# Seven block products instead of eight in one half of a feed-forward input projection

## The chip, the cores and the metric

The kernel runs on one NeuronCore of a Trainium2 chip as one launch. The metric is the device time of that launch in microseconds (us). Five engines run their own instruction streams in order and meet at semaphores: PE (TensorE, matrix products into PSUM), DVE (VectorE), ACT (ScalarE), POOL (GpSimd) and SP (SyncE, which here issues the DMAs of the weights).

## The reference, cut to what matters

Two blocks of layers work on 256 tokens of a sequence `x` and 256 tokens of a context, D_MODEL = 1024, in float32. The change lies in the second block, layer 1, in the first of its two feed-forward networks, which handles both token sets (512 columns):

```python
D_FF = 2816
def swiglu(h, w_in, w_out):
    a, b = jnp.split(h @ w_in, 2, axis=-1)
    return (jax.nn.silu(a) * b) @ w_out
...
x = x + 0.5 * mx[:, 2] * swiglu(ada_norm(x, norm_g[l, 0], mx[:, 0], mx[:, 1]), ffn_w_in[l, 0], ffn_w_out[l, 0])
hctx = hctx + 0.5 * mc[2] * swiglu(ada_norm(hctx, norm_g[l, 0], mc[0], mc[1]), ffn_w_in[l, 0], ffn_w_out[l, 0])
```

`h @ w_in` is 512 tokens by 1024 by 5632. The kernel computes it in two halves of 11 gate chunks (columns of `a`) and 11 value chunks (columns of `b`), 128 columns each, with the output projection of each half behind it.

## The kernel before, in words

A phase list (`plan`) is walked by each engine; a phase of kind `gemm` is one weight matrix or part of one. Everything is kept transposed: features on the 128 partitions, tokens along the free axis. `h` is 8 chunks of 128 features by 512 tokens (256 of x, then 256 of the context).

Every operand is split into two float32r parts, `hi` (a rounded copy) and `lo` (value minus `hi`), and a product is three matmuls: hi by hi, hi by lo, lo by hi. A *unit* is one 128-column weight chunk: SP loads it from DRAM (512 KB) into one of four slots of `deep`, ACT copies it to `w_hi` (L1398), DVE subtracts to get `w_lo` (L1875), PE uses it. `w_hi` and `w_lo` are rings of RING = 4 units; ACT and DVE work LEAD = 3 units ahead of PE.

In the phase that the change replaces (evacuation `swiglu`, 22 units, alternately gate and value), PE runs for each unit 8 chunks x 3 parts x 2 token halves = 48 matmuls of 128x256 (L1063). For a pair of units ACT takes the gate's silu out of PSUM (L1450), DVE multiplies it with the value's PSUM bank into `gt` (L1904), rounds that to `g_hi` (L1908) and subtracts to get `g_lo` (L1910); `g` feeds the output projection. POOL does nothing there. Engines run a hardware loop of four units per round.

Ahead of it stands the output projection of the first half (evacuation `resid`, 8 output chunks of two units with 6 and 5 chunks of `g`, 66 matmuls each, the result added into `resid` by DVE, L1917). Behind it stands the output projection of the second half, whose matmuls read `g` chunk 10 as the last of their first output chunk.

## Time and profile before

| | us |
|---|---|
| runs of the kernel before, median of 3 | 2347.16 (2341.73 to 2347.69) |
| the profiled execution, whole | 2344.51 |
| its span | 2342.7 |
| PE busy in the span | 2249.8 (96%) |
| DVE, ACT, POOL busy | 1144.3, 855.9, 176.3 |
| first half's output projection on PE | 1695.17 to 1755.13 = 59.96 |
| second half's input projection on PE (replaced) | 1755.13 to 1875.03 = 119.90 |

The profile is of one execution. Its page gives busy time by engine, a chain of what ended last, and groups of instructions by source line. The trace behind it answers for any stretch of time: busy time of each engine, instructions in order, and what an engine waited for. Line numbers are those of the kernel before.

### The profile page before, as it was taken

The page shows a single profiled execution, that of the slowest core. Times are in us where ns is not written, and L with a number is a line of the kernel's source. Part 1 is how long each engine was busy: PE and PEld are TensorE (multiplying, and loading weights), DVE is VectorE, ACT ScalarE, POOL GpSimd, SP SyncE. Part 2 cuts the span into 40 slices and gives each one's busy share as a digit, 9 for nine tenths or more (in the row PEclk, how much of TensorE's full clock was granted, in tenths as well). Part 3 has the DMA queues.
Part 4 walks back from the last instruction along what each step waited for, and adds up shares of the span by engine and source line. Part 5 has one row for each costly group of instructions (what it writes and reads, how often), then busy time and mean ns, then how long its engine had stood idle before and what let it go on. Part 6 is the DMA issues. An engine that isn't in the chain of part 4 may idle for free.

```text
span 2342.7 us, 47206 instructions
## 1 busy us (share of the span) xinstructions
PE 2249.8 (96%) x19336; PEld 2107.6 (90%) x19336; DVE 1144.3 (49%) x1926; ACT 855.9 (37%) x1392; POOL 176.3 (8%) x150
## 2 busy tenths in 40 slices
PE   6999999899999999988999999999999999999998
PEld 4986798789999999976999999999999998968998
DVE  5226375653433445456653333354343345576665
ACT  4125454632221233248432222243222234356544
POOL 0003112100000010501200000010000010001000
PEclk9999999999999999998999999999999998999999
DMA  9653544444675343521364665243243233324573
GB/s 309 193 160 112 156 142 107 122 149 152 182 213 179 89 131 115 154 73 28 109 183 127 204 199 175 84 118 91 72 122 93 82 98 91 91 64 128 172 209 111
DMA packets 515886, 315.53 MB, mean 135 GB/s; under 512 B 16035, under 2 KB 513274, under 8 KB 515622
## 3 DMA queue, kind: packets, MB, share of 16 engines
q1 hardware_dynamic: 515160, 313.45, 45.6%
q8 instruction: 99, 1.62, 0.3%
q14 instruction: 37, 0.30, 0.0%
q10 hardware_dynamic: 590, 0.16, 0.0%
HBM read 312.50 MB, written 1.06 MB: 134 GB/s over the span
## 4 chain that ended last, share of the span: by engine, by line
PE 87%; DVE 7%; ACT 3%; issue 2%; DMA 1%; ACTq 0%; POOL 0%; DVEq 0%; POOLq 0%
PE ps L1063 65%; PE ps L1107 4%; PE ps L796 3%; PE ps L1010 3%; DVE w_lo L1875 2%; PE ps L980 2%; ACT w_hi L1398 1%; PE ps L938 1%; PE ps L2142 1%; PE ps L2126 1%; PE ps L907 1%; PE ps L869 1%; PE ps L2490 1%; PE ps L2165 1%; PE ps L2394 0%
## 5 line engine op out<-in xcount | busy, mean ns | idle before, releaser
L1063 PE MATMUL ps<-h_hi,w_hi 128*128 128x256 f32 x3424 | 742.2, 282 | 11.1 <-issue 3.6
L1063 PE MATMUL ps<-h_lo,w_hi 128*128 128x256 f32 x3424 | 733.6, 279 | 0.0
L1063 PE MATMUL ps<-h_hi,w_lo 128*128 128x256 f32 x3424 | 733.0, 279 | 0.0
L1063 PEld LDWEIGHTS ps<-h_hi,w_hi 128*128 128x128 f32 x3424 | 548.4, 189 | 32.0 <-issue 26.5
L1063 PEld LDWEIGHTS ps<-h_lo,w_hi 128*128 128x128 f32 x3424 | 549.1, 190 | 0.1
L1063 PEld LDWEIGHTS ps<-h_hi,w_lo 128*128 128x128 f32 x3424 | 549.1, 190 | 0.0
L1875 DVE TENSOR_TENSOR w_lo<-stage,w_hi 128x1024 fp32r<-128x1024 f32 x227 | 285.3, 1259 | 264.2 <-ACT w_hi L1398 264.1
L1398 ACT ACTIVATE w_hi<-stage 128x1024 fp32r<-128x1024 f32 x227 | 236.5, 1055 | 337.3 <-PE ps L1063 217.3
L1875 DVE TENSOR_TENSOR w_lo<-deep,w_hi 128x1024 fp32r<-128x1024 f32 x184 | 225.2, 1234 | 236.9 <-ACT w_hi L1398 235.3
L1398 ACT ACTIVATE w_hi<-deep 128x1024 fp32r<-128x1024 f32 x184 | 190.9, 1055 | 157.1 <-PE ps L1063 116.0
L1063 PE MATMUL ps<-g_hi,w_hi 128*128 128x256 f32 x1100 | 233.8, 281 | 0.8 <-DVE w_lo L1875 0.3
L1063 PE MATMUL ps<-g_hi,w_lo 128*128 128x256 f32 x1100 | 231.4, 279 | 0.0
L1063 PE MATMUL ps<-g_lo,w_hi 128*128 128x256 f32 x1100 | 231.2, 279 | 0.0
L1450 ACT ACTIVATE vtok<-ps 128x512 f32<-128x512 f32 (+1 forms) x82 | 44.3, 540 | 475.1 <-PE ps L1063 475.1
L1063 PEld LDWEIGHTS ps<-g_hi,w_hi 128*128 128x128 f32 x1100 | 173.9, 188 | 5.9 <-issue 4.0
L1063 PEld LDWEIGHTS ps<-g_hi,w_lo 128*128 128x128 f32 x1100 | 174.0, 189 | 0.0
L1063 PEld LDWEIGHTS ps<-g_lo,w_hi 128*128 128x128 f32 x1100 | 173.5, 188 | 0.0
L1540 DVE TENSOR_REDUCE modT<-ps 128x16 f32 (+1 forms) x88 | 12.0, 171 | 218.3 <-PE ps L807 218.3
L1958 POOL MEMSET vtok<- 128x512 f32 x6 | 3.2, 527 | 1205.1 <-PE ps L1063 1205.1
L796 PE MATMUL ps<-modw,svec 128*32 128x256 f32 x1408 | 89.7, 386 | 0.0
L1904 DVE TENSOR_TENSOR vtok<-vtok,ps 128x512 f32<-128x512 f32 (+1 forms) x82 | 50.2, 612 | 73.8 <-PE ps L1063 73.8
L1917 DVE SCALAR_TENSOR_TENSOR resid<-ps,modA,resid 128x256 f32<-128x256 f32 (+1 forms) x120 | 53.5, 479 | 52.3 <-PE ps L1063 52.3
(406 smaller groups left out, 2896.4 us busy)
## 6 DMA issues: line engine op xcount, KB each, us to landing
modw<-in_ada_w SPq DMA_DIRECT2D x72, 1024.0 KB, 6.9
stage<-in_ffn_w_in SPq DMA_DIRECT2D x88, 512.0 KB, 3.9
deep<-in_ffn_w_in SPq DMA_DIRECT2D x88, 512.0 KB, 3.9
modw<-in_w_mod SPq DMA_DIRECT2D x18, 1024.0 KB, 8.3
stage<-in_w_in SPq DMA_DIRECT2D x30, 512.0 KB, 5.2
stage<-in_ffn_w_out SPq DMA_DIRECT2D x32, 384.0 KB, 3.3
stage<-in_even_w_in SPq DMA_DIRECT2D x24, 512.0 KB, 4.1
deep<-in_ffn_w_out SPq DMA_DIRECT2D x32, 384.0 KB, 3.3
```

Source lines behind the costliest of these rows:

```text
L796: last = mm(ps[32 * j:32 * j + 32, 4, 0:SEG], svec[:, m["block"], k, lhs], modw[:, par, k, :], start=par == 0 and k < 4, stop=par == 1 and ...
L869: last = mm(half_sums(v)[:, a * 64:(a + 1) * 64], part[:, a * P:(a + 1) * P], ones[:, 0:64], start=first and a + n == 0, stop=final and n ...
L907: last = mm(ps[:, k, cols], w_part[wp][:, (u0 + k) % RING, c, :], x_part[xp][:, c, cols], start=n == 0 and wp == xp, stop=n == KC - 1 and ...
L980: last = mm(ps[:, 2 + j, cols], w_part[wp][:, u % RING, n, :], t_part[xp][:, x, cols], start=x == 0 and wp == xp, stop=x == sum(ks) - 1 an ...
L1010: last = mm(ps[:, bank, part], w_part[wp][:, u % RING, n, :], x_part[xp][:, n, cols], start=n == 0 and wp == xp and (k["dst"] is not None ...
L1063: last = mm(ps[:, j, v - a:v - a + SEQ], w_part[wp][:, u % RING, c, :], x_part[xp][:, x, v:v + SEQ], start=first and wp == xp and v == a, ...
L1107: last = mm(ps[:, bank, (tile % 2) * SEQ:(tile % 2) * SEQ + SEQ], x_part[xp][:, c, tile * P:(tile + 1) * P], w_part[wp][:, u % RING:u % RI ...
L1398: up(act(w_hi[:, u % RING], slot, ACT.Copy), "w_hi", rounds)
L1450: up(act(sg[:, j // 2, 0:n], ps[:, j, 0:n], ACT.Silu), f"bank_free{j}", rounds)
L1875: up(V.tensor_tensor(w_lo[:, u % RING], arrival(u)[0], w_hi[:, u % RING].bitcast(F32), ALU.subtract), "w_ready", rounds)
L1904: up(V.tensor_tensor(gt[:, 0:n], sg[:, j // 2, 0:n], ps[:, j, 0:n], ALU.mult), f"bank_free{j}", rounds)
L1917: last = V.scalar_tensor_tensor(rs, ps[:, j, v * SEQ:(v + 1) * SEQ], gate[:, bass.ds(i * 8 + at, 1)], rs, ALU.mult, ALU.add)
```

## The change

The weights of one gate chunk and one value chunk form, with the two halves of the 1024 features, a 2 by 2 block matrix: A11 and A12 (gate; features 0 to 511, 512 to 1023), A21 and A22 (value). The tokens form B11, B12 (features 0 to 511 of x and of the context) and B21, B22. A block product is 128x512 by 512x256, 4 chunks x 3 parts = 12 matmuls. The plain result takes eight block products; the new phase `cells` takes seven, after Winograd's form of Strassen's product:

- weight sums, for each of 11 pairs, on POOL: S1 = A21 + A22, S2 = S1 - A11, S3 = A11 - A21 (written over A21 in its `deep` slot), S4 = A12 - S2;
- token sums, once, on POOL during the output projection ahead: T1 = B12 - B11, T2 = B22 - T1, T3 = B22 - B12, and T2 - B21 (`neg4`), each then split by ACT and DVE into hi and lo;
- products: A11 B11, S2 T2, A12 B21, S3 T3, S1 T1, S4 B22, A22 (T2 - B21, the sign taken up by the sums), some of them accumulated on one another in PSUM;
- result sums on ACT (one copy, `modr`) and DVE (five additions of 128x256 with one PSUM input). POOL multiplies silu(gate) with value in two halves of 128x256; ACT rounds to `g_hi`, DVE makes `g_lo`.

Each of the seven weight blocks of a pair is split by its own ACT copy and DVE subtraction (128x512), six products ahead of PE, in a ring of eight half units. `neg4`, the T2 parts and two of the sum buffers lie over tiles that are idle there; `wgate` moves into the shared stretch so that T3's hi part can lie over it. The semaphore `v_sb` is renamed `copied`. The output projection ahead now hosts the token sums and the first six weight splits, and is written out instead of looped, as is the new phase.

```diff
+BLOCKS_AHEAD = {(1, 2): (0, 1), (1, 3): (2, 3, 4, 5)}
+CELL_PRODUCTS = (("A11", 1, "B11"), ("S2", 2, "T2"), ("A12", 1, "B21"), ("S3", 3, "T3"), ("S1", 2, "T1"), ("S4", 2, "B22"), ("A22", 3, "N4"))
+CELL_ORDER = [(n + turn, x) for n in range(-1, FH) for x, turn in ((0, 1), (5, 0), (6, 0), (1, 1), (2, 1), (3, 1), (4, 1)) if 0 <= n + turn < FH]
...
+                elif half and (l, i) == (1, 0):
+                    n = len(CELL_ORDER)
+                    add("cells", {...}, w=w)
...
+                if not half and (l, i) == (1, 0):
+                    gemm(w_down.pop("w"), 0, KC, "resid", tok=(0, nt), fed=False, blocks=True,
+                         rises={"pre_added": 8, "hi_ready": 8 + 2 * LEAD, "h_ready": 8 + 2 * LEAD}, **w_down)
+                    continue
...
+        def sp_cells(eng, p):
+            for m in range(2 * FH):
+                u = p.at("unit_done") + m
+                slot, full, _, again = arrival(u)
+                eng.wait_ge(S("w_ready"), u - again + 1)
...
+        def pe_cells(eng, p):
...
+                eng.wait_ge(S("h_ready"), low_done(p, n, what))
...
+                if what == "S1":
+                    eng.wait_ge(S("half_evac"), p.at("half_evac", 5 * n + 1))
+                if what == "S4":
+                    eng.wait_ge(S("half_evac"), p.at("half_evac", 5 * n + 2))
+                if what == "A22":
+                    eng.wait_ge(S("half_evac"), p.at("half_evac", 5 * n + 3))
+                x_hi, x_lo = cell_operands(operand)
+                for c in range(4):
+                    for w_, x_ in ((hi, x_hi), (hi, x_lo), (lo, x_hi)):
+                        last = mm(ps[:, bank, 0:SEQ], w_[:, c, :], x_(c), start=..., stop=c == 3 and w_ is lo, skip_group_check=True)
...
+        def act_cells(eng, p):
...
+            def rounded(n):
+                eng.wait_ge(S("g_half"), p.at("g_half", 2 * n + 2))
+                up(act(g_hi[:, n, :], gt[:, :], ACT.Copy), "g_hi_ready")
...
+                if ahead < E:
+                    act_cell_high(eng, p, ahead)
...
+                if what == "S3" and n:
+                    rounded(n - 1)
...
+        def dve_cells(eng, p):
...
+                if ahead < E:
+                    dve_cell_low(eng, p, ahead)
+                    if CELL_PRODUCTS[CELL_ORDER[ahead][1]][0] == "A22":
...
+                        up(V.memset(tick[:, :], 0.0), "w_ready", by=2)
...
+                if what == "S1":
+                    product_done(eng, p, e)
+                    if n:
+                        eng.wait_ge(S("g_half"), p.at("g_half", 2 * n))
+                    up(V.tensor_tensor(out1, kept, q2, ALU.add), "half_evac")
...
+        def pool_cells(eng, p):
...
+            def sums(n):
...
+                up(G.tensor_tensor(s1, a21, a22, ALU.add), "pre_added")
...
+                up(G.tensor_tensor(s2, s1, a11, ALU.subtract), "pre_added")
+                up(G.tensor_tensor(a21, a11, a21, ALU.subtract), "pre_added")
...
+                up(G.tensor_tensor(s4, a12, s2, ALU.subtract), "pre_added")
...
+            def gated(n):
+                for v in range(2):
...
+                    up(G.tensor_tensor(gt[:, cols], sg[:, n % 2, cols], blocksum[3][:, cols], ALU.mult), "g_half")
...
+            for n in range(FH):
+                if n + 1 < FH:
+                    sums(n + 1)
+                if n:
+                    gated(n - 1)
+            gated(FH - 1)
```

On DVE, at the start of the second half's input projection, the kernel before has this in a row (the first two units' steps of a four-unit loop; ISA and REGISTER_ALU rows are loop bookkeeping and waits):

```order
L1875 TENSOR_TENSOR w_lo<-deep,w_hi 128x1024 [waits w_hi]
L1874 REGISTER_ALU
L1875 TENSOR_TENSOR w_lo<-deep,w_hi 128x1024 [waits w_hi]
L1900 REGISTER_ALU
L1902 REGISTER_ALU [waits unit_done]
L1903 ISA [waits bank_free0]
L1904 TENSOR_TENSOR vtok<-vtok,ps 128x512 [waits g_ready]
L1908 ISA [waits bank_free1]
L1908 COPY g_hi<-vtok 128x512
L1909 REGISTER_ALU
L1910 REGISTER_ALU [waits g_hi_ready]
L1910 TENSOR_TENSOR g_lo<-vtok,g_hi 128x512
```

The kernel after has this on DVE in the same projection, for one pair in the steady part (`blocksum_87`, `blocksum_88`, `convt` hold S1, S2, S4; `deep` a raw block or S3; `blocksum_89` the two halves of the value result, `dlam` and `modb` other result halves; `w_hi_90` and `w_lo_91` are the rings of eight half units):

```order
L2078 TENSOR_TENSOR blocksum_89<-modr,ps 128x256 [waits g_half,x_done]
L2080 TENSOR_TENSOR blocksum_89<-blocksum_89,ps 128x256 [waits half_evac]
L2053 TENSOR_TENSOR g_lo<-vtok,g_hi 128x512 [waits g_hi_ready]
L2042 TENSOR_TENSOR w_lo_91<-blocksum_87,w_hi_90 128x512 [waits hi_ready]
L2042 TENSOR_TENSOR w_lo_91<-deep,w_hi_90 128x512 [waits hi_ready]
L2087 TENSOR_TENSOR dlam<-modr,ps 128x256 [waits sg_half,x_done]
L2042 TENSOR_TENSOR w_lo_91<-convt,w_hi_90 128x512 [waits hi_ready]
L2093 TENSOR_TENSOR blocksum_89<-modb,ps 128x256 [waits g_half,half_evac,x_done]
L2042 TENSOR_TENSOR w_lo_91<-deep,w_hi_90 128x512 [waits hi_ready]
L2064 MEMSET tick 128x1 [waits h_ready]
L2073 TENSOR_TENSOR modb<-modr,ps 128x256 [waits half_evac,copied,x_done]
L2042 TENSOR_TENSOR w_lo_91<-blocksum_88,w_hi_90 128x512 [waits hi_ready]
```

Two wide subtractions, a multiplication, a rounding and a subtraction for a pair have become seven subtractions of half the width, five additions that wait for products, `g_lo`, and a one-element memset (`tick`) that tells SP that two `deep` slots are free.

On POOL the kernel before has no instruction in this projection; the kernel after has this for each pair in the steady part:

```order
L2302 TENSOR_TENSOR blocksum_87<-deep 128x512 [waits h_ready,deep_full3,deep_full2]
L2306 TENSOR_TENSOR blocksum_88<-blocksum_87,deep 128x512 [waits h_ready,pre_added]
L2307 TENSOR_TENSOR deep<-deep 128x512
L2311 TENSOR_TENSOR convt<-deep,blocksum_88 128x512 [waits h_ready,pre_added]
L2319 TENSOR_TENSOR vtok<-vtok,blocksum_89 128x256 [waits g_ready,half_evac,sg_half] x2
```

The four sums for pair n + 1 stand in front of the two halves of the g product of pair n - 1 (`vtok<-vtok,blocksum_89`).

## Rows read from the trace of the kernel before

**Rows 1.** The page: span, PE's busy row, and the chain that ended last

```profile
span 2342.7 us, 47206 instructions
PE 2249.8 (96%) x19336; PEld 2107.6 (90%) x19336; DVE 1144.3 (49%) x1926; ACT 855.9 (37%) x1392; POOL 176.3 (8%) x150
...
PE 87%; DVE 7%; ACT 3%; issue 2%; DMA 1%; ACTq 0%; POOL 0%; DVEq 0%; POOLq 0%
PE ps L1063 65%; PE ps L1107 4%; PE ps L796 3%; PE ps L1010 3%; DVE w_lo L1875 2%; PE ps L980 2%; ACT w_hi L1398 1%; PE ps L938 1%; PE ps L2142 1%; PE ps L2126 1%; PE ps L907 1%; PE ps L869 1%; PE ps L2490 1%; PE ps L2165 1%; PE ps L2394 0%
```

**Rows 2.** Stretches of PE's stages before: busy us of each engine, clock, DMA

```profile
core 0: us, PE busy (x) PEld busy (x) DVE busy (x) ACT busy (x) POOL busy (x), PEclk, DMA share, GB/s
1695.17:1755.13 59.96, 59.96 (x528) 59.96 (x529) 28.59 (x34) 17.79 (x17) 0.00 (x0) 1.00 0.39 114
1755.13:1875.03 119.90, 119.84 (x1058) 119.68 (x1057) 43.34 (x53) 27.30 (x33) 0.00 (x0) 1.00 0.31 88
1875.03:1928.11 53.08, 53.08 (x451) 53.08 (x452) 25.95 (x30) 19.55 (x23) 8.99 (x8) 1.00 0.36 102
2236.68:2296.81 60.13, 60.00 (x530) 59.80 (x528) 36.84 (x53) 24.89 (x33) 0.00 (x0) 1.00 0.67 189
2064.00:2104.00 40.00, 38.36 (x240) 26.14 (x240) 26.41 (x61) 14.86 (x33) 1.81 (x1) 1.00 0.14 41
1060.00:1100.00 40.00, 34.29 (x195) 27.69 (x194) 26.07 (x68) 31.61 (x105) 6.37 (x5) 0.87 0.05 14
```

**Rows 3.** Costliest DVE groups by shape: count, busy us, mean ns, idle before

```profile
L1875 DVE TENSOR_TENSOR w_lo<-deep,w_hi 128x1024 fp32r<-128x1024 f32 x184 | 225.2, 1234 | 236.9 <-ACT w_hi L1398 235.3
...
L1910 DVE TENSOR_TENSOR g_lo<-vtok,g_hi 128x512 f32 x54 | 37.4, 692 | 6.6
...
L1904 DVE TENSOR_TENSOR vtok<-vtok,ps 128x256 f32<-128x256 f32 x22 | 9.1, 414 | 0.0
```

**Rows 4.** ACT groups by shape, same columns

```profile
L1406 ACT ACTIVATE h_hi<-mixT 128x512 fp32r<-128x512 f32 x20 | 11.5, 624 | 6.5 <-DVE mixT L2770 3.2 <-DVE mixT L2317 3.1
...
L1450 ACT ACTIVATE vtok<-ps 128x256 f32<-128x256 f32 x22 | 8.4, 382 | 33.1 <-PE ps L1063 33.0
```

**Rows 5.** POOL groups by shape, same columns

```profile
L1965 POOL TENSOR_TENSOR vtok<-vtok 128x512 f32<-128x512 f32 x24 | 31.0, 1290 | 128.1 <-ACT vtok L1175 113.0 <-issue 15.1
...
L2002 POOL TENSOR_TENSOR vtok<-vtok 128x256 f32<-128x256 f32 x8 | 5.9, 735 | 68.9 <-ACT vtok L1317 68.9
```

**Rows 6.** Timeline of DVE: start us, duration us, instruction, idle before it

```profile
275.24 1.23 DVE L1875 TENSOR_TENSOR w_lo<-wgate,w_hi 128x1024 fp32r<-128x1024 f32 x1 [8.64 <-ACT w_hi L1398]
...
278.63 0.41 DVE L1529 TENSOR_TENSOR modr<-ps,modb 128x256 f32<-128x256 f32 x1
...
1129.26 1.23 DVE L1875 TENSOR_TENSOR w_lo<-stage,w_hi 128x1024 fp32r<-128x1024 f32 x1 [0.26 <-ACT w_hi L1398]
...
1134.16 1.53 DVE L1875 TENSOR_TENSOR w_lo<-stage,w_hi 128x1024 fp32r<-128x1024 f32 x1 [1.65 <-ACT w_hi L1398]
```

**Rows 7.** Timeline of POOL in the same two stretches

```profile
275.77 1.86 POOL L1976 TENSOR_TENSOR vtok<-vtok 128x512 f32<-128x512 f32 x1 [9.32 <-ACT vtok L1175]
277.93 1.93 POOL L1976 TENSOR_TENSOR vtok<-vtok 128x512 f32<-128x512 f32 x1 [0.30 <-ACT vtok L1175]
...
1133.31 1.29 POOL L1965 TENSOR_TENSOR vtok<-vtok 128x512 f32<-128x512 f32 x1 [1.12 <-issue]
```

**Rows 8.** The page: GB/s in 40 slices, and one DMA group's time to landing

```profile
GB/s 309 193 160 112 156 142 107 122 149 152 182 213 179 89 131 115 154 73 28 109 183 127 204 199 175 84 118 91 72 122 93 82 98 91 91 64 128 172 209 111
...
deep<-in_ffn_w_in SPq DMA_DIRECT2D x88, 512.0 KB, 3.9
```

More of the change, by code:

```diff
@@ L1127, in pe_gemm, with cell_entry @@
                         pe_extra(eng, p, j)
+        def cell_entry(p, e):
+            n, x = CELL_ORDER[e]
+            what = CELL_PRODUCTS[x][0]
+            gate, value = (arrival(p.at("unit_done") + 2 * n + m)[0] for m in range(2))
+            src = {"A11": gate[:, 0:4, :], "A12": gate[:, 4:8, :], "S3": value[:, 0:4, :], "A22": value[:, 4:8, :]}.get(what)
+            if src is None:
+                src = blocksum[{"S1": 0, "S2": 1, "S4": 2}[what]][:, :].rearrange("p (c n) -> p c n", n=P)
+            if e == len(CELL_ORDER) - 1:
+                return n, what, src, last_w[0][:, :, :], last_w[1][:, :, :]
+            slot = (2 * p.at("unit_done") + e) % (2 * RING)
+            return n, what, src, w_hi8[:, slot], w_lo8[:, slot]
@@ L1478, in act_gemm, with act_blocks, act_cell_high @@
                         act_extra(eng, p, j)
+        def act_blocks(eng, p, q):
+            eng.wait_ge(S("pre_added"), p.at("pre_added", 4 * q + 4))
+            rows = slice(2 * q, 2 * q + 2)
+            for n, out in enumerate((h_hi[:, rows, SEQ:NT], wide[0][:, rows, :], diff_hi[:, rows, :], neg4[0][:, rows, :])):
+                up(act(out, halves(blocksum[(0, 2, 3, 1)[n]][:, :]), ACT.Copy), "hi_ready")
+        def act_cell_high(eng, p, e):
+            n, what, src, hi, _ = cell_entry(p, e)
+            if what[0] == "A":
+                full, arrived = arrival(p.at("unit_done") + 2 * n + (what == "A22"))[1:3]
+                eng.wait_ge(full, arrived)
+            else:
+                eng.wait_ge(S("pre_added"), p.at("pre_added", 4 * n + int(what[1])))
+            if e == len(CELL_ORDER) - 1:
+                eng.wait_ge(S("h_ready"), low_done(p, n, "S4"))
+            elif e < 2 * RING:
+                eng.wait_ge(S("unit_done"), p.at("unit_done", e // 2 - RING + 1))
+            else:
+                eng.wait_ge(S("x_done"), p.at("x_done", e - 2 * RING + 1))
+            up(act(hi, src, ACT.Copy), "hi_ready")
@@ L2010, in pool_gemm @@
         def pool_gemm(eng, p):
             k = p.kw
+            if k.get("blocks"):
+                pool_blocks(eng, p)
             if k["evac"] == "post":
```

213 lines of the change are left out of this document (203 added, 10 removed).

## The prediction

> **What bounds the kernel now.** I read the page first. PE is busy for 96% of the span and carries 87% of the chain that ended last, 65% of it in line 1063 [rows 1]. So a matmul removed counts in full, as long as nobody else becomes late in that place. Then I asked for the busy time of the engines in the three stages around the change [rows 2]. In the replaced projection PE is busy for 119.84 of 119.90 us, DVE for 43.3, ACT for 27.3, POOL for none, and the clock is at full speed (1.00, the 2.4 GHz level). The reader is to see there that PE alone sets the time of that stage, and that three engines have room. The last views are of the room: what one instruction of the new kinds takes [rows 3 to 5], and what happens where DVE and POOL work side by side [rows 6, 7].
>
> **PE.** 22 units x 48 matmuls = 1056 in 119.90 us are 0.1135 us each [rows 2]. Seven products of 12 for each of 11 pairs are 924; 132 go, 15.0 us. The new matmuls add 12 times in a row to one PSUM region of 256 columns. The last feed-forward does so too (256 tokens only): its 528 matmuls took 60.13 us, 0.1139 each [rows 2], so that costs nothing. PE alone would need 104.9 us for the stage, 9.54 per pair against 10.90.
> The pitch is not always that: the output projection behind ran 451 records in 53.08 us, 0.1177 each [rows 2]. I don't know what picks one of the two. For the 528 matmuls ahead of the stage a change of pitch would cost 2.2 us, behind the stage it would give as much back. I take 0 and keep +/-2 for the range.
>
> **The room of each engine, per pair (11 pairs).**
> - ACT: seven splits and g_hi, 8 x 0.624 (a 128x512 copy out of SBUF), and one copy and two silu of 128x256, 3 x 0.382 [rows 4]: 6.1 us. It fits in 9.54.
> - DVE: seven splits and g_lo, 8 x 0.692, and five additions with one PSUM input, 5 x 0.414 [rows 3]: 7.6 us, with the memset some 7.7. What goes is two wide splits, a multiplication, a rounding and g_lo, some 4.3.
> - POOL: four sums of 128x512, 4 x 1.290, two g halves, 2 x 0.735 [rows 5]: 6.6 us, where there was nothing.
> Each fits. Together DVE and POOL do not.
>
> **DVE beside POOL.** At 1134.16 DVE starts a w_lo while POOL has an addition running (1133.31, 1.29 us). It takes 1.53 us, its like five microseconds earlier 1.23 [rows 6, 7]. So it really began at 1134.16 + 0.30 = 1134.46, 0.14 before POOL's end at 1134.60. The other way round: DVE's w_lo of 275.24 ends at 276.47; POOL's addition of 275.77 takes 1.86 instead of 1.29, so began at 276.34, 0.13 before DVE's end. Neither shares: the later one stands until the earlier is nearly through. The addition at 278.63 with its input in PSUM takes its normal 0.41 in the middle of a POOL instruction (277.93, 1.93 us), so only DVE's instructions with both inputs in SBUF are caught.
> That makes one resource of the two. Held time per pair: POOL 4 x (1.29 - 0.14) + 2 x (0.735 - 0.14) = 4.60 + 1.19; DVE 8 x (0.69 - 0.13) = 4.48. Sum 10.3 us, over PE's 9.54. The period of a pair can't be below 10.3.
> The Trainium skill has this as a rule, in "SBUF — State Buffer", section "SBUF: two separate sides": the port pair that DVE and GpSimd share is an exclusive lock, held for the whole instruction, and the loser fully blocks. The rows agree, but for the last 0.13 to 0.14 us of an instruction. With whole instructions, as the page says, the sum would be 4 x 1.29 + 2 x 0.735 + 8 x 0.69 = 12.2 us per pair, and the time by the formula below about 2354.
>
> **Where the resource stands idle.** DVE can't start a pair's first result half (`out1`) before POOL's second g half, and in front of that addition stands the split of the next S3 block, whose hi part ACT makes only behind `rounded`, which waits for the same g half. So once a pair: g half done, ACT rounds (0.62), ACT copies S3 (0.62), DVE subtracts. That is 1.25 us in which DVE has nothing for the shared path. Can POOL use it? Its next sums need both weight blocks of the pair, whose DMAs go out at `tick`. One lands after 3.9 us; the second moves 512 KB more, at the 309 GB/s of the page's busiest slice 1.7 us [rows 8]: 5.6 us behind the tick. Between tick and the end of the g halves lie an addition, two subtractions that each wait for POOL, and POOL's last sum and g halves: 0.41 + 2 x 0.56 + 1.15 + 1.19 = 3.9 us. So POOL waits for its data just while DVE waits for ACT, and I take the 1.25 as idle, mostly: 1.3 with the semaphores. Bounds: 0 if POOL fills it (10.3 per pair); from above a serial chain, given as rival C. I take 11.6, near the low one because most of DVE's additions do lie beside POOL's held time.
>
> **The sum.** The first pair finds six splits made and the last one no sums beside it; both run at PE's pace. Between them are 8 periods from tick to tick at which DVE and POOL set the pace: 8 x (11.6 - 9.54) = 16.5 us. The last pair's S4 and A22 products each wait for an addition (0.41 and the matmul's own tail), 0.6 each. Stage: 104.9 + 16.5 + 1.2 = 122.6 against 119.9: +2.7 us.
> General form: change = 8 x (period - 9.54) - 13.8.
> The projection ahead (59.96 us, DVE busy 28.6 [rows 2]) takes on 18 token sums and the first pair's 4 weight sums on POOL, 22 x 1.29 = 28 us; 14 splits more on DVE (9.7 us) and ACT (8.7 us). The shared path there: 22 x 1.15 + 14 x 0.56 + 16 wide splits of 1.1 = 51 of 60 us. It fits, and a split that comes late by one POOL instruction (1.15 us) is covered by the three units (some 11 us) that DVE is ahead of PE. ACT waits at its third output for POOL's first nine sums: 9 x 1.15 and five wide splits between them, 16 us, before its turn at about 20. Price: 0. Without that cover ACT, and three units later PE, would wait for what is missing; I allow 2 us.
> The clock: PE will stand still for about 2 us per pair in short waits. In 2064 to 2104 PE's weight loads fill 26 of 40 us and the clock stays 1.00, in 1060 to 1100 28 of 40 and it is 0.87 [rows 2]. Should it fall, PE still has the 2 us of slack per pair to lose first. Price 0.
> Total +2.7. The profiled execution would go from 2344.51 to 2347.2; the runs of before have a median of 2347.16, 2.65 higher, so on their scale I get 2349.9, about 2350.
>
> **Rivals.**
> - A, the forecast: shared path plus the hand-over through ACT. Periods of 10.8 to 12.1 us give -3.7 to +6.7: 2343 to 2354.
> - B, PE keeps the pace. DVE and POOL would have to interleave without meeting, or the stalls seen with 1024-wide splits would not come with 512-wide ones. For it: each engine alone has 1.9 us of room or more, and work stands six products ahead. Against it: both sides of the stall are in the rows, and ahead-work covers a late instruction, not a rate. Time: -15.0 us, 2332; with the slow pitch for 924 matmuls (+3.9) 2336. Between A and B lies the packed path, 10.3 per pair: 8 x 0.76 - 13.8 = -7.7, 2339.5.
> - C, slower: the loop through SP and POOL closes late. From `tick`: weights 5.6; four sums, each with a subtraction of DVE in front, 4 x 1.71 = 6.8; two g halves likewise 2.3; ACT twice 1.25; subtraction and two additions 1.5; then g_lo, three splits and the last one, each behind a POOL instruction, 5 x 1.71 = 8.6; two additions and tick 1.0: 27.0 us for two pairs, 13.5 per pair. With none of them blocked it is 5.6 + 5.2 + 1.5 + 1.25 + 1.5 + 3.5 + 1.0 = 19.5, 9.8 per pair. It decides over A where more than half of those meetings happen in series; from a period of 12.1 on the kernel is slower by over 0.3% (8 x 2.6 - 13.8 = +7). Halfway between A and its end, 12.8: +12.3, 2359.5. For it: every engine is in order, and each of DVE's waits for POOL delays the tick. Against it: blocked time on one side is working time of the other.
> That the products don't drop from eight to seven can't be: the order of instructions has 12 matmuls for each.
>
> **Chances.** 0.3% of 2347 is 7 us, about what a measurement of this kernel tells from no change. A 0.52 (within 0.3% but for 0.08 slower and 0.02 faster); B 0.14, faster; the packed path 0.08, of which 0.06 faster; C 0.26, of which 0.24 slower. Sum: faster 0.22, same 0.46, slower 0.32. The time is A's, 2350. The range goes down to B with the slow pitch, 2336, and up past C's middle to 2362; outside are some 0.12 below and 0.08 above.
>
> **What would show it.** The stage on PE (from the first matmul of the new line after 1755 to the first g matmul) takes 118 to 126 us; below 112 speaks for B, above 127 for C. PE's idle time in it, about 16 us, is ended by DVE: by the addition `blocksum_89<-modr,ps` or `modb<-modr,ps`, not by a DMA. DVE's 128x512 subtractions average well over 0.69, near 1.1, and POOL's sums over 1.29, while DVE's additions stay at 0.41. `tick` to `tick` is about 11.6 us, perhaps uneven in turn. Once a pair DVE waits for ACT `w_hi` behind `g_hi`. The stage ahead stays within 2 us of 59.96. Wrong would be the whole account if the subtractions stay at 0.69 beside POOL; wrong in size if POOL fills the hand-over, or if its sums wait for DMAs long after that.

## The result, and the profile after

| | before | changed |
|---|---|---|
| median (range), us | 2345.15 (2340.09 to 2351.62), 6 runs | 2360.1 (2356.85 to 2365.16), 6 runs |
| ratio, 95% interval | | 1.0069 [1.0053, 1.0084] |
| profiled execution / its span, us | 2344.51 / 2342.7 | 2360.34 / 2358.6 |

The change makes the kernel slower, by 0.7%. The time lies inside the forecast range of 2336 to 2362 and above the forecast 2350. The range reached that far only because it took in rival C; against the runs of before that were measured beside it the kernel is 15.0 us slower, and A's own bounds were -3.7 to +6.7. What happened is nearer rival C than A.

The page after, against [rows 1]:

```profile
span 2358.6 us, 47189 instructions
PE 2244.2 (95%) x19204; PEld 2097.1 (89%) x19204; DVE 1214.0 (51%) x2033; ACT 893.2 (38%) x1489; POOL 301.2 (13%) x234
...
PE 81%; DVE 8%; ACT 3%; issue 3%; POOL 2%; DMA 1%; ACTq 0%; DVEq 0%; SPq 0%; POOLq 0%
```

The 132 matmuls are gone, and PE's share of the chain that ended last fell from 87% to 81%: POOL and DVE took places in it. Next the stretches of PE's three stages, as in [rows 2]: the projection ahead, the changed one, the projection behind. The fourth row is five pairs out of the middle of the changed stage, from one S2 sum of POOL to the fifth after it:

```profile
1697.22:1757.19 59.97, 59.97 (x529) 59.97 (x529) 42.65 (x45) 22.33 (x28) 40.12 (x23) 1.00 0.34 96
1757.19:1893.82 136.63, 114.55 (x926) 112.88 (x925) 100.42 (x151) 60.06 (x118) 82.98 (x59) 0.96 0.32 89
1893.82:1957.07 63.25, 63.25 (x540) 63.20 (x539) 29.19 (x37) 24.10 (x30) 10.47 (x10) 1.00 0.33 92
1781.66:1844.77 63.11, 51.60 (x411) 50.77 (x410) 46.82 (x71) 27.40 (x55) 42.40 (x30) 0.95 0.31 84
```

The loss is all in the changed stage: 136.63 against 119.90 us, +16.7. The stage ahead kept its 59.96, with all the token sums in it. (The profiled totals differ by 15.8; what is upstream of the stages ran 2.0 us longer, the rest 2.9 shorter. The start of the stage moves by several us between the profiled executions below, so these two say nothing.) A pair takes 63.11 / 5 = 12.6 us. No engine is busy for all of that: PE 82%, DVE 74%, POOL 67%. So the engines wait for one another. The view of waits in this stage names it (engine, line, releaser: us in total, times, longest):

```profile
POOL blocksum L2302 <- DVE w_lo L2042: 32.5, 8, 4.1
ACT g_hi L1634 <- POOL vtok L2319: 28.2, 9, 3.5
DVE w_lo L2042 <- ACT w_hi L1616: 25.3, 13, 2.5
PE ps L1231 <- DVE blocksum L2078: 22.1, 10, 2.9
...
ACT w_hi L1616 <- POOL blocksum L2306: 18.3, 9, 3.0
...
POOL blocksum L2302 <- DMA deep<-in_ffn_w_in: 5.7, 1, 5.7
```

Everyone waits for somebody in a circle (a round, in what follows), and the DMA hardly has a part. The costliest groups of DVE and POOL in the stage, against [rows 3, 5]:

```profile
L2042 DVE TENSOR_TENSOR w_lo<-deep,w_hi 128x512 fp32r<-128x512 f32 x39 | 41.7, 1072 | 24.1 <-ACT w_hi L1616 24.1
...
L2078 DVE TENSOR_TENSOR blocksum<-modr,ps 128x256 f32<-128x256 f32 x11 | 4.6, 415 | 0.6 <-PE ps L1231 0.6
...
L2319 POOL TENSOR_TENSOR vtok<-vtok,blocksum 128x256 f32<-128x256 f32 x20 | 19.6, 1000 | 7.6 <-DVE blocksum L2093 7.6
L2311 POOL TENSOR_TENSOR convt<-deep,blocksum 128x512 f32<-128x512 f32 x10 | 17.4, 1738 | 0.0
...
L2302 POOL TENSOR_TENSOR blocksum<-deep 128x512 f32<-128x512 f32 x9 | 14.5, 1612 | 38.2 <-DVE w_lo L2042 32.5 <-DMA deep<-in_ffn_w_in 5.7
```

A splitting subtraction takes 1.03 us on the mean of all 70 (1.07 in the largest group) instead of 0.69, a sum 1.6 to 1.74 instead of 1.29: they hold one another. The addition with a PSUM input keeps its 0.415. One turn of the round, in the timelines of POOL, ACT and DVE (start, duration):

```profile
1799.38 1.88 POOL L2319 TENSOR_TENSOR vtok<-vtok,blocksum 128x256 f32<-128x256 f32 x2
1805.33 1.59 POOL L2302 TENSOR_TENSOR blocksum<-deep 128x512 f32<-128x512 f32 x1 [4.07 <-DVE w_lo L2042]
```

```profile
1801.30 0.63 ACT L1634 ACTIVATE g_hi<-vtok 128x512 fp32r<-128x512 f32 x1 [2.18 <-POOL vtok L2319]
1801.84 0.61 ACT L1616 ACTIVATE w_hi<-deep 128x512 fp32r<-128x512 f32 x1
```

```profile
1802.48 0.69 DVE L2042 TENSOR_TENSOR w_lo<-deep,w_hi 128x512 fp32r<-128x512 f32 x1 [2.51 <-ACT w_hi L1616]
1803.09 0.41 DVE L2078 TENSOR_TENSOR blocksum<-modr,ps 128x256 f32<-128x256 f32 x1
1803.54 0.42 DVE L2080 TENSOR_TENSOR blocksum<-blocksum,ps 128x256 f32<-128x256 f32 x1
1803.88 0.68 DVE L2053 TENSOR_TENSOR g_lo<-vtok,g_hi 128x512 fp32r<-128x512 f32 x1
1804.48 0.68 DVE L2042 TENSOR_TENSOR w_lo<-blocksum,w_hi 128x512 fp32r<-128x512 f32 x1
```

POOL ends g at 1801.26. ACT rounds g, then copies S3; DVE splits S3, adds twice (PE stands ahead of its S4 product and waits for the first of them, 1.29 us this time), makes g's low part and splits the S1 sum; only then may POOL write its next S1 sum into the same buffer, at 1805.33. From g's end to there POOL stands still for 4.07 us, in most pairs, and its train of four sums and two g halves takes the other 8.5.

POOL's stand-still isn't idle time of the path that DVE and POOL share: in it DVE makes three subtractions of 0.68 to 0.69. Nobody uses the path from g's end to the S3 split, 1801.26 to 1802.48, and from that split's end to g's low part, 1803.17 to 1803.88, while DVE makes its two additions: 1.22 and 0.71 us. I laid the timelines of DVE's subtractions and of POOL over one another for six pairs (S2 sum 1781.66 to 1857.37): per pair the path is busy for 10.7 us and idle for 1.9, together 12.6, and the idle time is these two gaps again and again.

### The profile page after: what moved, and what is told of

Read it like the earlier page. It is cut to its first block, busy times and chain, and to the rows that moved or that the text cites. A ratio compares the mean times of both kernels' runs of the same rounds, so it can differ in the third digit from the quotient of the medians.

```text
span 2358.6 us, 47189 instructions
## 1 busy us (share of the span) xinstructions
PE 2244.2 (95%) x19204; PEld 2097.1 (89%) x19204; DVE 1214.0 (51%) x2033; ACT 893.2 (38%) x1489; POOL 301.2 (13%) x234
## 4 chain that ended last, share of the span: by engine, by line
PE 81%; DVE 8%; ACT 3%; issue 3%; POOL 2%; DMA 1%; ACTq 0%; DVEq 0%; SPq 0%; POOLq 0%
PE ps L1097 59%; PE ps L1141 4%; PE ps L830 3%; PE ps L1044 3%; DVE w_lo L2126 2%; PE ps L1014 2%; ACT w_hi L1508 1%; PE ps L972 1%; PE ps L2447 1%; PE ps L2463 1%; POOL vtok L2319 1%; POOL convt L2311 1%; POOL blocksum L2302 1%; PE ps L903 1%; DMA wgate<-in_w_out 1%
## 5 line engine op out<-in xcount | busy, mean ns | idle before, releaser
L1097 PE MATMUL ps<-h_hi,w_hi 128*128 128x256 f32 x3072 | 673.2, 282 | 11.9 <-DVE w_lo L2126 3.8
L1097 PE MATMUL ps<-h_lo,w_hi 128*128 128x256 f32 x3072 | 664.7, 279 | 0.0
L1097 PE MATMUL ps<-h_hi,w_lo 128*128 128x256 f32 x3072 | 663.9, 279 | 0.0
L1097 PEld LDWEIGHTS ps<-h_hi,w_hi 128*128 128x128 f32 x3072 | 494.9, 190 | 32.7 <-issue 26.8
L1097 PEld LDWEIGHTS ps<-h_lo,w_hi 128*128 128x128 f32 x3072 | 495.7, 190 | 0.1
L1097 PEld LDWEIGHTS ps<-h_hi,w_lo 128*128 128x128 f32 x3072 | 495.6, 190 | 0.0
L2126 DVE TENSOR_TENSOR w_lo<-deep,w_hi 128x1024 fp32r<-128x1024 f32 x162 | 205.8, 1282 | 165.5 <-ACT w_hi L1508 162.4
L1508 ACT ACTIVATE w_hi<-deep 128x1024 fp32r<-128x1024 f32 x159 | 165.2, 1055 | 120.3 <-PE ps L1097 78.2
L1565 ACT ACTIVATE vtok<-ps 128x512 f32<-128x512 f32 (+1 forms) x71 | 37.7, 531 | 401.8 <-PE ps L1097 401.7
L2176 DVE COPY big<-ps 128x512 f32<-128x512 f32 (+1 forms) x34 | 19.7, 580 | 104.5 <-PE ps L1097 104.4
```

What stands on the lines that cost most here:

```text
L1097: last = mm(ps[:, j, v - a:v - a + SEQ], w_part[wp][:, u % RING, c, :], x_part[xp][:, x, v:v + SEQ], start=first and wp == xp and v == a, ...
L1508: up(act(w_hi[:, u % RING], slot, ACT.Copy), "w_hi", rounds)
L1565: up(act(sg[:, j // 2, 0:n], ps[:, j, 0:n], ACT.Silu), f"bank_free{j}", rounds)
L2126: up(V.tensor_tensor(w_lo[:, u % RING], arrival(u)[0], w_hi[:, u % RING].bitcast(F32), ALU.subtract), "w_ready", rounds)
```

## The experiments

All figures of a stage are from the profiled run; "five pairs" is the stretch from one S2 sum to the fifth after it. A ratio is against runs of the kernel before made beside that kernel (medians 2339.4 to 2343.1), so compare ratios rather than microseconds.

### Which wait closes the round: g first, or a second buffer

In the first kernel POOL multiplies g ahead of its sums.

```diff
             for n in range(FH):
-                if n + 1 < FH:
-                    sums(n + 1)
                 if n:
                     gated(n - 1)
+                if n + 1 < FH:
+                    sums(n + 1)
```

> GpSimd multiplies g of pair n-1 before it sums the weight blocks of pair n+1 (in the changed kernel it does so behind them); no other instruction is changed. Theory H (hand-over): in the changed kernel a pair takes 12.55 us because GpSimd's first sum waits until VectorE has split the previous S1 sum, which stands behind g's second half, ScalarE's rounding, two additions and g's low part: 4 us in which GpSimd stands still each pair. With g first that round is cut, a pair takes 9.6 to 10.8 us, the stage 106 to 118 us, the kernel 2331 to 2343 us. Theory X (the SBUF exclusion of VectorE and GpSimd alone sets the pace): the work of both is unchanged, so a pair still takes 11.6 us or more, the kernel 2352 to 2361 us.

Measured: 1.0118 [1.0099, 1.0137], 2366.87 us, five pairs in 68.74 us, 13.7 each. The forecast of H is missed on the wrong side, and X's 2352 to 2361 too, though the wait that H named is gone (stretch of the stage, and waits of POOL and of PE):

```profile
1754.63:1898.21 143.58, 118.62 (x927) 116.94 (x926) 91.02 (x151) 57.78 (x118) 73.05 (x59) 0.93 0.31 85
```

```profile
POOL vtok L2319 <- DVE blocksum L2093: 63.7, 10, 7.1
```

```profile
PE ps L1231 <- DVE blocksum L2078: 25.0, 10, 2.5
```

POOL now waits for out0, that is for PE's A22 product, and does nothing meanwhile. DVE and POOL meet less (S1 sums of 1283 ns), and the round is no shorter for it. That it is longer goes with the clock. Two pairs in a row, from tick to tick:

```profile
1821.58:1834.16 12.58, 10.04 (x86) 9.88 (x86) 8.38 (x14) 5.34 (x11) 7.22 (x7) 1.00 0.31 85
1834.16:1848.29 14.13, 11.60 (x87) 11.43 (x86) 8.47 (x14) 5.23 (x11) 7.24 (x7) 0.88 0.27 74
```

Where the clock stays at 1.00 the pair takes 12.6 us as in the changed kernel; where it falls behind PE's gap, PE is busy for 1.6 us more, in the S4 and A22 products of which POOL waits for the last, and the pair takes 14.1.

In the second kernel S1 has two buffers in pairs 3 to 10 (the second one is a free slot of `g_hi`), the wait looks two pairs back.

```diff
-                if n:
-                    eng.wait_ge(S("h_ready"), low_done(p, n - 1, "S1"))
+                if n:
+                    eng.wait_ge(S("h_ready"), low_done(p, n - (2 if n > 2 else 1), "S1"))
```

> The S1 sum alternates between two buffers in pairs 3 to 10 (a free slot of g is the second), so GpSimd's first sum no longer waits for VectorE's split of the pair before; the order of GpSimd's work is the changed kernel's. Theory H: in these eight pairs the 4 us stand-still shrinks to what the next buffers (S2, S4) allow, a pair takes 10.3 to 11.5 us instead of 12.55, the kernel 2344 to 2353 us. Theory X: nothing moves, 2357 to 2363 us.

Measured: 1.0060 [1.0039, 1.0081], 2358.0 us. A pair takes some 15 and 9.4 us in turn from tick to tick, so only an even number tells the pace: six pairs, from S2 sum to S2 sum, took 71.77 us, 12.0 each. H's range for the kernel (2344 to 2353) is missed again, and X's (2357 to 2363) is met. In the profiled run the stage is 4.4 us shorter, 132.2 us; the ratio, 1.0060 against 1.0069, doesn't tell that from nothing. POOL's wait shrank from 32.5 to 18.9 us, and DVE's splits grew from 1072 to 1159 ns: most of what was standing still became holding.

### How much is the contention

Two kernels leave out most of one side's work and keep every wait. The first sums only 8 of each 128 columns on POOL (`s1[:, :, 0:8]` and so on in the four sums):

> GpSimd's four sums of a pair cover 8 of each 128 columns; the rest of each sum is left out. All waits stay. Theory P (TensorE keeps its pace once it is fed): a pair takes 9.54 us, the stage 105 to 107 us, the kernel 2330 to 2334 us. Both H and X say this too. Rival: the seven products have a cost of their own (the waits of S4, A22 and S1 on VectorE's additions), then a pair stays over 10.3 us and the kernel over 2339 us.

Measured: 0.9963 [0.9949, 0.9976], 2331.54 us. The second splits only 8 of each 128 columns on DVE:

```diff
+            w = 8 if 16 <= e < len(CELL_ORDER) - 1 else P
-            up(V.tensor_tensor(lo, src, hi.bitcast(F32), ALU.subtract), "h_ready")
+            up(V.tensor_tensor(lo[:, :, 0:w], src[:, :, 0:w], hi.bitcast(F32)[:, :, 0:w], ALU.subtract), "h_ready")
```

> VectorE's seven splitting subtractions of a pair cover 8 of each 128 columns from the third pair on; the rest of the low parts is left out. GpSimd's work, the buffers and all waits stay. Theory X: GpSimd is no longer held, its sums fall from 1.60 to 1.74 us to 1.29 and its products from 1.00 to 0.74, its train of a pair to 6.7 us, under TensorE's 9.54: the kernel comes to 2331 to 2335 us. Theory H: the train shrinks as much, but the stand-still behind ScalarE's rounding, the additions and g's low part stays at 2.8 to 3.3 us: 9.6 to 10.2 us a pair, 2332 to 2339 us. In both GpSimd's durations show what the exclusion costs; only its idle time tells them apart.

Measured: 0.9985 [0.9972, 0.9998], 2334.94 us. The stage in the first and in the second, and the S2 sum of the second:

```profile
1753.08:1862.55 109.47, 107.03 (x927) 106.86 (x925) 82.66 (x151) 60.26 (x118) 32.18 (x57) 1.00 0.40 111
```

```profile
1755.11:1866.91 111.80, 108.51 (x926) 107.67 (x925) 67.25 (x151) 60.78 (x118) 66.51 (x59) 1.00 0.39 109
...
L2307 POOL TENSOR_TENSOR blocksum<-blocksum,deep 128x512 f32<-128x512 f32 x10 | 13.3, 1329 | 0.8
```

P holds for the kernel's time (2330 to 2334). PE is busy without a gap from its first S3 product (1757.24) to its last (1854.30); these ten pairs take 97.06 us, 9.71 each and not 9.54, and the stage takes 109.47, over P's 105 to 107. With DVE's splits short the same order and buffers give 9.8 us a pair, and POOL still stands still behind DVE five times, at most 3.1 us: its train is so much shorter that PE sets the pace. X and H had both forecast this time. So each side's work is needed for the loss. But a shortened side holds nobody and is also quicker itself, so these two kernels don't show how much of a pair is holding and how much is plain length. X alone falls short in any case: both engines' held time, 10.3 us, is not the 12.6 that a pair took.

### Who stands ahead of the addition that PE waits for

In each step DVE did a split for the product six ahead and then the addition that is due. The next kernel turns this round, on ACT too, the one after it also puts g first on POOL.

```diff
             for e in range(E):
-                ahead = e + 2 * LEAD
-                ... split(ahead)
                 ... the additions of product e
+                ahead = e + 2 * LEAD
+                ... split(ahead)
```

> GpSimd's order is the changed kernel's. At each step VectorE first does the additions of that product and then the splitting subtraction for the product six ahead, and ScalarE first its copy, silu or rounding and then its copy for the product six ahead; in the changed kernel the work ahead stands first. Theory O (order): the round is TensorE's S4 product behind VectorE's first addition to out1, that addition behind a split for a product six ahead, and the split behind GpSimd's sums; work ahead is put before work that is due. With the due work first the additions come out of that round, but g still stands behind the sums: 10.8 to 12.2 us a pair, the kernel 2344 to 2357 us. Theory X (the exclusion of VectorE and GpSimd sets the pace at about 11.6 us or more): no gain, 2352 to 2361 us.

> The same, and GpSimd multiplies g of the pair before ahead of its sums, as in the run that came out at 13.9 us a pair. Theory O: with both orders turned no engine waits for work that is due later; what is left is VectorE's and GpSimd's held time, 10.3 us, and its rough edges: 10.2 to 11.0 us a pair, the stage 112 to 120 us, the kernel 2335 to 2346 us, and TensorE's 2.7 us gap ahead of the S4 product, with the half clock behind it, is gone. Theory X: the pace stays at 11.6 us or more, 2352 us or more. If g first is bad by itself, whatever the order of the additions, a pair stays near 13.9 us and the kernel near 2367 us.

Measured: 1.0102 [1.0071, 1.0132], 2368.23 us (12.9 a pair), and 1.0118 [1.0089, 1.0147], 2371.97 us (13.6). Theory O in this form is wrong: no gain. The first is over X's range too; the second fits X, which had no upper end there, and comes nearest to the third case of its expectation, g first bad by itself. PE still waits for the same addition (L2069 here), 22.3 and 23.4 us. The second kernel's timeline of DVE shows why:

```profile
1801.52 1.10 DVE L2042 TENSOR_TENSOR w_lo<-blocksum,w_hi 128x512 fp32r<-128x512 f32 x1 [3.01 <-ACT w_hi L1616]
1802.56 1.74 DVE L2042 TENSOR_TENSOR w_lo<-deep,w_hi 128x512 fp32r<-128x512 f32 x1
1804.22 0.41 DVE L2069 TENSOR_TENSOR blocksum<-modr,ps 128x256 f32<-128x256 f32 x1
```

Putting the addition first inside its own step helps nothing: ahead of it stand the steps before, with the splits of S2 and A12 of the next pair, which PE uses four and five products later. The first of them waits 3.01 us (for ACT's copy of it, which waits for a POOL sum), the second is held by another. Here too the clock adds to it, in two pairs in a row from tick to tick:

```profile
1812.24:1824.59 12.35, 9.97 (x87) 9.81 (x86) 8.76 (x14) 5.35 (x12) 7.67 (x7) 1.00 0.30 86
1824.59:1838.56 13.97, 11.59 (x87) 11.42 (x86) 8.89 (x15) 5.34 (x12) 7.68 (x7) 0.88 0.28 76
```

So it was the distance, not the order within a step, that I tried next. It is three products instead of six in the next kernel; the one after it gives g's product to DVE too, with silu's result in a PSUM bank.

```diff
-                ahead = e + 2 * LEAD
+                ahead = e + 3
-                if ahead < E:
+                if 2 * LEAD <= ahead < E:
```

> As the run with both orders turned (g first on GpSimd, due work first on VectorE and ScalarE), and the weight blocks are split three products ahead instead of six. Theory O, sharpened: what closed the round at 13.9 us in the last two runs is the first addition to out1 on VectorE, which stands behind the splits of S2 and A12 of the next pair although those are needed 4 to 5 products later; these wait for GpSimd's sums, which wait for g, which waits for the A22 product of the pair before. With three products ahead these splits stand behind the addition. Then 10.3 us (both engines' held time) to 11 us a pair, the stage 113 to 120 us, the kernel 2336 to 2346 us, TensorE without its 2.5 us gap ahead of S4. Theory X: 11.6 us or more, 2352 us or more. If the splits come too late with three products ahead, TensorE stands before S2 or A12 instead of S4 and the kernel stays over 2355 us.

> The same, but g's product of a pair is made by VectorE (two of 128x256), with silu's result read from a PSUM bank; GpSimd makes only the four sums. Its held time falls from 5.8 to 4.6 us a pair, and operations with a PSUM input were not held at all, so the two engines' held time is 9.1 us, under TensorE's 9.54; VectorE's own busy time is 8.4 us. Theory O: TensorE's pace or just above it, 9.54 to 10.3 us a pair, the stage 105 to 113 us, the kernel 2330 to 2338 us, and faster than the run beside it. Theory X in its strict form (held time counts wherever it stands): also faster than the run beside it by about 1 us a pair, 10 us in all, but from 11.6, so 10.6 us a pair and 2342 us.

Measured: 1.0031 [1.0017, 1.0045], 2349.54 us, and 1.0019 [1.0005, 1.0033], 2346.82 us. PE's waits in the first:

```profile
PE ps L1231 <- DVE w_lo L2042: 11.7, 9, 1.4
PE ps L1231 <- DVE blocksum L2069: 1.5, 2, 1.1
```

The wait for the addition went from 23.4 to 1.5 us and the pair from 13.6 to 11.7 (11.57 in steady state). It is one edit, so it is shown that the distance caused that wait. It also took away the long gap ahead of S4, and with it the low clock; of the 2 us a pair only some 0.8 (12.35 to 11.57) are left where the clock is full in both. Laid over one another as above, the path of DVE and POOL is busy for 10.6 us of a pair here and idle for 1.0. The size that O gave (10.3 to 11) is not reached, and X's 11.6 a pair is met (its 2352 us isn't); for the second kernel both theories had forecast less (at most 10.6 us a pair) and both are missed. Both kernels have the same 11.57 although POOL's work differs by two g halves; DVE is busy for 50.31 and 53.11 us of five pairs, and in the second POOL waits 50.2 us for weights:

```profile
1785.87:1844.17 58.30, 51.56 (x422) 49.45 (x420) 50.31 (x71) 27.76 (x55) 43.62 (x30) 1.00 0.34 91
```

```profile
1783.61:1842.58 58.97, 51.58 (x422) 49.43 (x422) 53.11 (x81) 27.32 (x55) 31.98 (x21) 1.00 0.33 90
...
L2323 POOL TENSOR_TENSOR blocksum<-deep 128x512 f32<-128x512 f32 x9 | 12.9, 1437 | 50.2 <-DMA deep<-in_ffn_w_in 50.2
```

### DVE's own load, or the round through the weights

The next kernel asks for the gate block's weights early, and its distance is four.

```diff
-                    if CELL_PRODUCTS[CELL_ORDER[ahead][1]][0] == "A22":
-                        m = CELL_ORDER[ahead][0]
-                        eng.wait_ge(S("h_ready"), low_done(p, m, "A22"))
-                        up(V.memset(tick[:, :], 0.0), "w_ready", by=2)
+                    m, freed = CELL_ORDER[ahead][0], CELL_PRODUCTS[CELL_ORDER[ahead][1]][0]
+                    if freed in ("A12", "A22"):
+                        eng.wait_ge(S("h_ready"), low_done(p, m, freed))
+                        eng.wait_ge(S("pre_added"), p.at("pre_added", 4 * m + 4))
+                        up(V.memset(tick[:, :], 0.0), "w_ready")
```

> As the run with g on VectorE, but the blocks are split four products ahead, and a weight slot is given back to the DMAs as soon as it is free: the gate block's after A12 is split and S4 summed, the value block's after A22 is split; before, both waited for A22's split. Theory R (a round through the DMA): in the last two runs a pair took 11.57 us with g on GpSimd as with g on VectorE, so the engines' work did not set it; tick to landed weights is 6.2 us, then the A11 split of that pair, which the A22 split of the pair before follows in VectorE's fixed order, each held by a GpSimd sum that starts at the same landing (1.3 to 1.7 us each, three of them), then the next tick. With the gate block asked for some 9 us earlier the round is open: 10.0 to 11.0 us a pair, the stage 110 to 120 us, the kernel 2333 to 2342 us. Theory X (VectorE's own time with what holds it is the bound: its rows add up to 11.4 us of 11.57 in that run): 11.4 us or more a pair, 2345 us or more.

Measured: 0.9978 [0.9963, 0.9994], 2337.3 us, faster than before; five pairs in 52.75 us (10.55 each), DVE busy for 49.22 of them. That is inside R's range; but the edit changed two things. Next DVE is relieved: the A11 product is copied by ACT into the bank where S2 accumulates, without a `start` on S2, and ACT reads the middle sums out. The same edit also puts g's product into PSUM, so that its low part has a PSUM input, and makes the distance five; the diff shows only the copies and additions.

```diff
-                    up(act(modr[:, n % 2, :], ps[:, n % 2, 0:SEQ], ACT.Copy), "copied")
+                    up(act(ps[:, 6 + n % 2, 0:SEQ], ps[:, n % 2, 0:SEQ], ACT.Copy), "copied")
+                if what == "S2":
+                    up(act(modb[:, :], ps[:, 6 + n % 2, 0:SEQ], ACT.Copy), "copied")
+                if what == "S1":
+                    up(act(modr[:, n % 2, :], ps[:, 6 + n % 2, 0:SEQ], ACT.Copy), "copied")
-                    up(V.tensor_tensor(out1, kept, q2, ALU.add), "half_evac")
-                    up(V.tensor_tensor(out1, out1, q3, ALU.add), "half_evac")
+                    up(V.tensor_tensor(out1, kept, q3, ALU.add), "half_evac")
-                    up(V.tensor_tensor(dlam[:, :], kept, q2, ALU.add), "half_evac")
```

(The Trainium skill, "PSUM — Partial Sum Buffer", section "Specifications (TRN2)", says that VectorE may take one tensor input from PSUM at most; that is why ACT, and not the addition itself, reads the second bank. No run here shows what two would do.)

> The same, five products ahead, and VectorE relieved: ScalarE copies the A11 product into the PSUM bank in which S2, S1 and S4 accumulate, so three of VectorE's five additions of a pair go (1.24 us), against two more ScalarE copies of 128x256 (0.37 us each) for the middle sum and for out1; g's product is written to PSUM, so that its low part has a PSUM input and is not held. VectorE's own time is then 8 x 0.69 + 4 x 0.41 = 7.2 us a pair, the held time 4.6 + 7 x 0.56 = 8.5 us, ScalarE's 6.8 us, all under TensorE's 9.54. Theories R and X both say TensorE's pace or near it: 9.5 to 10.3 us a pair, the stage 105 to 113 us, the kernel 2330 to 2337 us. If it stays over 10.8 us a pair, there is another round that neither names.

Measured: 0.9946 [0.9929, 0.9963], 2329.55 us, just under its forecast of 2330. Then the same with both blocks asked for together, and the changed kernel with the early request alone:

> As the run with the A11 product kept in the accumulating bank, but a pair's two weight blocks are asked for together behind A22's split, as in the changed kernel. Theory R (the round through the DMA is a limit of its own): tick to landed weights 6.2 us, ScalarE's copy of A11 0.6, then the splits of A11, S4 and A22, each held by one of the sums that start at the same landing (1.1 to 1.7 us each), and the next tick: 10.8 to 11.5 us a pair, the kernel 2338 to 2346 us, however little VectorE has to do. Theory X (with 7.2 us of its own work VectorE is no limit): as the run with two ticks, about 10.0 us a pair and 2329 us.

> The changed kernel with nothing else altered than the early request for the gate block. My rival C had the changed kernel's period set by the loop tick, weights landed, sums, g, ScalarE, additions; in its trace GpSimd waited only 5.7 us in all for weights. Theory H/O (the orders on GpSimd, ScalarE and VectorE close the round at 12.55 us, and the DMA has slack there): no change, 12.4 to 12.6 us a pair, 2355 to 2362 us. Theory C as predicted (the landing weights are in the round): about 1 us a pair less, 2346 to 2352 us.

Measured: 0.9949 [0.9932, 0.9965], 2329.92 us, and 1.0065 [1.0047, 1.0083], 2355.44 us: X met in the first, H/O in the second. Five pairs in the kernel with the relieved DVE and two ticks, with one tick, and in the changed kernel with two:

```profile
1777.93:1827.80 49.87, 49.87 (x431) 49.71 (x430) 49.17 (x71) 30.79 (x67) 31.58 (x21) 1.00 0.37 107
```

```profile
1778.75:1826.81 48.06, 48.06 (x418) 48.06 (x417) 40.44 (x66) 30.93 (x65) 31.71 (x21) 1.00 0.41 111
```

```profile
1776.16:1839.08 62.92, 53.15 (x421) 52.31 (x421) 48.99 (x76) 27.62 (x55) 42.19 (x30) 0.95 0.29 85
```

PE is called busy for every microsecond of the first two, but only the one-tick kernel runs at PE's own pace: from its first S3 product to its last ten pairs take 97.06 us, 9.71 each, to the hundredth what the kernel with short sums took. (From S2 sum to S2 sum it is 9.6, since POOL makes up for its late start.) With two ticks PE keeps 9.71 for five pairs and then takes 9.96; from S3 product to S3 product, the two halves:

```profile
1759.80:1808.33 48.53, 48.53 (x422) 48.53 (x421) 44.83 (x68) 29.44 (x64) 28.33 (x19) 1.00 0.37 110
1808.33:1858.11 49.78, 49.73 (x423) 49.08 (x422) 49.25 (x74) 29.94 (x65) 29.82 (x19) 1.00 0.34 98
```

In the second half DVE is busy for 49.25 of 49.78 us: it sets the pace, and PE has used up its lead. Theory R falls as a limit of its own: with one tick the pair takes 9.7, not 10.8 or more. In the changed kernel the early request doesn't move the pair either (12.6 to 12.6), nor the time beyond its interval. The early request even brings contention: with it POOL's sums meet more of the splits, and DVE is busy for 49.2 of 49.9 us instead of 40.4 of 48.1. Whether the weights had a part in the 11.57 us of the two kernels with distance three stays open: the kernel that asked early also had distance four. Nor do the runs part the three things in the step from 10.55 to PE's pace (additions off DVE, g's product in PSUM, distance five).

Both last candidates beat the kernel before by 0.5% (12 to 13 us) and the changed one by about 1.2%.

## Why the prediction was right or wrong

- **PE's own need, 104.9 us, 9.54 a pair.** Nearly right: 9.71 where it is fed, 1.9 us more for the stage and inside the 2 us that were kept for the pitch. Five of the seven products go at the pitch that I took, two don't (below).
- **DVE and POOL share one path; additions with a PSUM input are free of it.** Right, with the sizes: subtractions 1.03 (near 1.1 forecast), sums 1.6 to 1.74, additions 0.41 to 0.42. Rival B fell with it.
- **"Price: 0" of the stage ahead.** Right: 59.97 us.
- **The hand-over, "I take the 1.25 as idle".** This is the step that failed. I asked when POOL's next *data* would be there (the weights, 5.6 us behind the tick) and not when its next *buffer* would be free. The S1 sum waits for DVE's split of the S1 sum before it, and this stands behind ACT's rounding, ACT's copy, a split, two additions and g's low part: POOL stands still for 4.07 us. In the trace the first sum starts 8.6 us after its tick (1796.71 to 1805.33), and POOL waited for weights once. The 1.25 us itself was right (1.22 measured); what I had at nothing is the second gap of the shared path, 0.71 us, in which DVE adds and POOL may not write. And the held time is 10.7, not 10.3. With 10.3 + 1.3 I had 11.6 us a pair; it is 10.7 + 1.9 = 12.6.
- **Nor is that wait the cause by itself,** as I thought at first behind the result: with the buffer doubled the pair takes 12.0, with the order turned 12.6 at full clock and 13.7 on the mean. Held steps and in-order queues close the next round at once. What lay in nearly all of them is the out1 addition, due now, behind splits that are due four to six products later. The prediction counted this distance as cover ("work stands six products ahead"). With g and the additions first, the runs show that it was the trouble for PE's wait (23.4 to 1.5 us when it is halved). In the changed kernel's own order the distance was never altered, so that it is the cause there is argued, not shown.
- **"8 periods".** Too few. From the first tick (1760.9) to the last (1883.1) are ten, 122.2 us against 95.4 at PE's pace, +26.8, where 8 periods of 12.6 give 24.5; ahead of the first and behind the last it is 14.4 us against 9.5, +4.9, where I had 1.2. My form gives +10.7 for 12.6 us a pair; the stage took +16.7, and of these 6.0 us the two ends make 3.7.
- **The clock, "price 0".** Right for the round of the changed kernel, and for the reason given: a pair with the clock at 0.86 took 12.58 us from S2 sum to S2 sum, one at 1.00 took 12.59 (below). PE lost idle time, not the pair. It isn't general: with g first the same fall costs some 1.5 us a pair. Whether the last fall, near 1880, lengthened the stage's end stays open.
- **Rival C.** Right in sign and nearly in size (2359.5 against 2360.1), and it was given 0.26. Its loop was another: it went through the DMA, and the early request shows that the DMA has no part. Its 2359.5 stood for a period of 12.8, a midpoint between A's bound and its own chain of 13.5, so that the number came so close is luck.
- **"PE idle, about 16 us, ended by DVE `blocksum<-modr,ps`".** The releaser right, the size 22.1. The stage's 136.6 us lie over the 127 that were to speak for C.

## What to carry to other kernels

Before an engine gets work that crosses to others, write down for each of its instructions what *frees its output buffer*, not only what brings its input, and follow that back through the in-order queues; a round shows itself where no engine is busy for all of the period. Where two engines share a path, ask of each stand-still of one whether the other uses the path in it: only the time in which neither does adds to the held time. Work done ahead on an engine that also has due work is cover only as long as it never waits: where its inputs come late, try a shorter distance. And in such a round taking away one wait, however large in the view of waits, may gain nothing or lose. What helped here was the shorter distance (2 us a pair, more than half of it by way of the clock), and for the last 0.8 us relieving DVE, through which all the chains pass, together with the edits made beside it; then distance five did no harm. Compare pairs at the same granted clock before you give a difference to an edit.

## What the runs showed of the hardware

**The shared path.** DVE's splits cut to 32 columns each bring POOL's sum back from 1606 to 1329 ns with nothing else altered: the 0.3 us belonged to DVE. The Trainium skill, "SBUF — State Buffer", section "SBUF: two separate sides", has the path as exclusive, and these runs agree in that each side lengthens the other's instructions. The rows don't bear out whole instructions, which would be 12.2 us held per pair: the path was busy for 10.7.

**The clock behind a gap.** In the changed kernel PE stood still ahead of the S4 products, 22.1 us in ten gaps, the longest 2.9. Behind that longest one (in the first row) the granted clock stayed at 1.00; behind the next, of 2.5 us, it was at the 1.2 GHz level for some three microseconds (0.52 of full speed in the last row), with 16 matmuls in 3.3 us instead of 28:

```profile
1773.00:1778.30 5.30, 2.40 (x22) 2.22 (x21) 2.77 (x4) 2.34 (x5) 2.93 (x3) 1.00 0.48 132
1778.30:1781.50 3.20, 3.19 (x27) 3.20 (x28) 3.20 (x6) 1.70 (x4) 1.51 (x1) 1.00 0.00 0
1786.00:1790.90 4.90, 2.38 (x21) 2.20 (x21) 2.36 (x4) 2.34 (x5) 2.53 (x3) 0.98 0.70 188
1790.90:1794.20 3.30, 3.29 (x16) 3.30 (x17) 2.47 (x6) 0.93 (x3) 1.56 (x1) 0.52 0.02 5
```

The first row has the 2.9 us gap, the third the 2.5 us one. The pair did not get longer by it; from S2 sum to S2 sum, one pair with the low clock and one without:

```profile
1781.66:1794.24 12.58, 10.04 (x74) 9.88 (x73) 9.04 (x15) 4.84 (x10) 8.44 (x7) 0.86 0.32 85
1807.00:1819.59 12.59, 9.98 (x85) 9.81 (x85) 9.88 (x15) 5.57 (x11) 8.45 (x7) 1.00 0.30 85
```

With g first it fell in most pairs, and the whole stage is at 0.93.

**Two pitches.** In both kernels that keep PE fed for the whole stage, every S3 product (moving tile `diff`) takes 1.44 us and all but one S2 product (`wide`) 1.42 for their 12 matmuls at full clock, while the five products over the other tiles take 1.36 to 1.38 in the steady part; in the one-tick kernel an S3 product runs from 1788.22 to 1789.66 and an A22 product from 1793.76 to 1795.12. So the pitch, 0.118 to 0.120 or 0.113 to 0.115 us, goes with the product and not with the kernel or the stretch. What it is about these two tiles no run here shows.
